# Moving work across tile borders in the first phase of a hybrid decoder layer

## The reference

```
h = rmsnorm(x, g_mix)                       # x * rsqrt(mean(x^2) + eps) * g
z = h @ w_in                                # split into xa, ga, q, k, v (512 columns each)
xa_c = causal_dwconv(xa_ext, conv_a_w, conv_a_b)            # width 4
r, gi = sigmoid(block_diag(xa_c, w_r, b_r)), sigmoid(block_diag(xa_c, w_i, b_i))
a = exp(-8 * r * softplus(-lambda))
u = sqrt(1 - a^2) * gi * xa_c;   hs = scan(h[t] = a[t] * h[t-1] + u[t])
ya = hs * gelu(ga);   q, k = partial_rope(q), partial_rope(k)
```

## Time and profile before

| | |
|---|---|
| median of 3 runs | 3018.76 us (3014.42 to 3021.68) |
| span of the profiled execution | 3016.2 us; its own time outside the profiler is not given, the span is 2.6 us under the median |
| mean granted TensorE clock | 0.969 of full speed |
| TensorE matmul busy | 2880.6 us (96%) |
| VectorE, ScalarE, GpSimd busy | 1738.7 (58%), 1482.5 (49%), 850.4 us (28%) |
| first phase: tile 0 of chunk 0 to the last turn of v | 18.4 to 591.5 us |

### The profile page before, as it was taken

The page is one execution under the profiler, slowest core; times in us unless marked ns, Lnnn a source line. Parts: engine busy times, 40 slices in busy tenths (PEclk is TensorE's granted clock), DMA queues, the critical chain, the costliest instruction groups (busy, mean ns, idle before and its releaser), DMA issues.

```text
span 3016.2 us, 44469 instructions
## 1 busy us (share of the span) xinstructions
PE 2880.6 (96%) x15264; PEld 2717.8 (90%) x15264; DVE 1738.7 (58%) x2949; ACT 1482.5 (49%) x2648; POOL 850.4 (28%) x960
## 2 busy tenths in 40 slices
PE   7898899999999998999999999999999999999998
PEld 6898898867666897999999999999999999999998
DVE  7867767689622675555546555455554555545543
ACT  5565655666655783554334443344433443344431
POOL 4566665545200244111321112111221112211111
PEclk8999999989899998999999999999999999999999
DMA  5344343455444333434434344343533444334332
GB/s 163 98 155 138 109 148 123 139 199 187 156 140 142 102 120 127 119 114 144 131 118 136 113 149 126 113 142 112 155 122 108 145 132 139 114 113 144 114 119 75
DMA packets 151107, 395.26 MB, mean 131 GB/s; under 512 B 19605, under 2 KB 66581, under 8 KB 146821
## 3 DMA queue, kind: packets, MB, share of 16 engines
q1 hardware_dynamic: 114480, 349.69, 37.0%
q10 hardware_dynamic: 34196, 34.58, 3.7%
q0 software_dynamic: 2240, 8.52, 0.7%
HBM read 358.17 MB, written 34.57 MB: 130 GB/s over the span
## 4 chain that ended last, share of the span: by engine, by line
PE 83%; DVE 5%; issue 5%; POOL 2%; ACT 2%; DMA 0%; DVEq 0%; POOLq 0%; ACTq 0%; SPq 0%
PE bank L1523 22%; PE bank L1525 22%; PE bank L1524 22%; PE bank L1594 7%; PE bank L1619 2%; PE bank L1606 2%; PE bank L1682 2%; PE bank L1618 1%; DVE xc L934 1%; DVE pm L1010 0%; DVE d L959 0%; PE bank L1678 0%; PE bank L1679 0%; DVE h_lo L870 0%; POOL sq L1288 0%
## 5 line engine op out<-in xcount | busy, mean ns | idle before, releaser
L857 DVE TENSOR_TENSOR w_lo<-stage,w_hi 128x1024 fp32r<-128x1024 f32 x500 | 652.3, 1305 | 348.0 <-ACT w_hi L471 340.3
L1523 PE MATMUL bank<-hb_hi,w_hi 128*128 128x416 f32 x2240 | 792.4, 354 | 21.4 <-DVE hb_lo L1163 20.2
L471 ACT ACTIVATE w_hi<-stage 128x1024 fp32r<-128x1024 f32 x500 | 527.7, 1055 | 548.8 <-PE bank L1525 529.9
L1525 PE MATMUL bank<-hb_hi,w_lo 128*128 128x416 f32 x2240 | 794.0, 354 | 0.0
L1524 PE MATMUL bank<-hb_lo,w_hi 128*128 128x416 f32 x2240 | 786.1, 351 | 0.0
L1523 PEld LDWEIGHTS bank<-hb_hi,w_hi 128*128 128x128 f32 x2240 | 423.4, 189 | 30.3 <-issue 16.9
L1524 PEld LDWEIGHTS bank<-hb_lo,w_hi 128*128 128x128 f32 x2240 | 424.0, 189 | 7.6 <-issue 0.6
L1525 PEld LDWEIGHTS bank<-hb_hi,w_lo 128*128 128x128 f32 x2240 | 422.9, 189 | 3.0
L1523 PE MATMUL bank<-ff_hi,w_hi 128*128 128x416 f32 x960 | 338.0, 352 | 0.0
L1525 PE MATMUL bank<-ff_hi,w_lo 128*128 128x416 f32 x960 | 337.3, 351 | 0.0
L1524 PE MATMUL bank<-ff_lo,w_hi 128*128 128x416 f32 x960 | 335.4, 349 | 0.0
(11 more groups left out here) (246 smaller groups left out, 4275.0 us busy)
## 6 DMA issues: line engine op xcount, KB each, us to landing
stage<-in_w SPq DMA_DIRECT2D x500, 512.0 KB, 3.6
past<-in_past SPq DMA_DIRECT2D x32, 1152.0 KB, 6.1
vb<-out_v SPq DMA_DIRECT2D x48, 256.0 KB, 2.8
attention_rows<-ob SPq DMA_DIRECT2D x32, 264.0 KB, 2.1
oc<-attention_rows SPq DMA_DIRECT2D x16, 528.0 KB, 3.9
xs<-in_x ACTq DMA_DIRECT2D x40, 208.0 KB, 2.5
qb<-query_rows SPq DMA_DIRECT2D x16, 512.0 KB, 7.8
xT<-in_x ACTq DMA_DIRECT2D x4, 1664.0 KB, 10.1
```

What stands on the lines that cost most here:

```text
L471: e.activation(w_hi[s][:], stage[s % STAGE][:], ACT.Copy).then_inc(hi_ready, 1)
L857: e.tensor_tensor(w_lo[s][:], stage[s % STAGE][:], w_hi[s][:].bitcast(F32), ALU.subtract).then_inc(lo_ready, 1)
L1523: e.matmul(out, w_hi[s][:, k], hi, start=start, stop=False)
L1525: return e.matmul(out, w_lo[s][:, k], hi, start=False, stop=stop)
```

## The change

Only the first phase is touched. The arithmetic is the same, and no DMA is added or taken away.

- TensorE: in tile 19 each step k but the last adds to a new semaphore `h_free`. The gate matmuls of group j stand behind tile 5j+3 instead of 5j+2, and `mean_square` behind tile 13 instead of 11.
- ScalarE: `normed_hi_a` of the next chunk stands, all eight slices together, ahead of group 3's square root (it was behind it, in two parts around the copy of `v_cols`). Slice k waits for `h_free` of step k, the last for the end of tile 19. The copies of q and k out of PSUM stand ahead of the sigmoids, and the root of the norm goes behind group 2's square root.
- VectorE: the scan of group j goes behind `xc_lo` of group j+1 (that of group 3 to the end of the chunk). In group 3, `ahead(c, v_t)` and all eight `normed_lo_a` stand ahead of the reciprocal of `d`; they were behind `a_`. The reciprocal of `rstd` goes to the end of group 2.
- GpSimd: the squares go behind the products that give `gi` of groups 0 and 1.

```
 ScalarE, normed_hi_a                      (h_free is a new semaphore)
                 for k in ks:
                     e.wait_ge(hn_ready, KD * c + k + 1)
+                    if not (isinstance(c, int) and c == 0):
+                        if k < KD - 1:
+                            e.wait_ge(h_free, (KD - 1) * (c - 1) + k + 1)
+                        else:
+                            e.wait_ge(tile_done, c * W_IN)
                     e.activation(h_hi[:, k], xT[:, k], ACT.Identity, ...)
 ScalarE, chunk
-                    if j == 2 and more:
-                        ... (root of the norm into rstd)
                     for i, t in enumerate(qk):
                         ahead(c, t)
+                        b = done(c, t)
+                        if not (first and j == 0):
+                            e.wait_ge(shuffled, 2 * m + i - 1)
+                        e.activation(raw[i][:], b[:, 0:C], ACT.Copy)...
                         if i == 1:
                             e.wait_ge(gates_done, m + 1)
                             ... (sigmoids and tanh)
-                        b = done(c, t)
-                        ... (the copy into raw[i])
                     ahead(c, v_t)
+                    if j == 3 and more:
+                        normed_hi_a(c + 1, range(KD))
                     e.wait_ge(d1_ready, m + 1)
                     e.activation(r_[:], r_[:], ACT.Sqrt, scale=4.0)...
+                    if j == 2 and more:
+                        ... (root of the norm into rstd)
                     b = done(c, v_t)
-                    if j == 3 and more:
-                        normed_hi_a(c + 1, range(3))
                     e.activation(v_cols[:], b[:, 0:C], ACT.Copy)...
-                    if j == 3 and more:
-                        normed_hi_a(c + 1, range(3, KD))
 VectorE, chunk
                     e.tensor_tensor(xc_lo[:], ...)
+                    if j > 0:
+                        scan(c, first, j - 1)
                     ...
                             e.tensor_scalar(d_[j % 2][:], r_[:], 1.0, None, ALU.add)...
                             e.wait_ge(d1_ready, m + 1)
+                            if j == 3 and more:
+                                ahead(c, v_t)
+                                normed_lo_a(c + 1, range(KD))
                             e.reciprocal(d_[j % 2][:], d_[j % 2][:])...
                             ...
-                        if i == 0 and j == 2 and more:
-                            ... (reciprocal of rstd)
-                    if j == 3 and more:
-                        normed_lo_a(c + 1, range(2))
-                    ahead(c, v_t)
-                    if j == 3 and more:
-                        normed_lo_a(c + 1, range(2, KD))
-                    ... (the scan, moved unchanged into scan(c, first, j))
+                    if not (j == 3 and more):
+                        ahead(c, v_t)
+                    if j == 2 and more:
+                        ... (reciprocal of rstd)
+                scan(c, first, JT - 1)
 GpSimd, chunk
-                    if more and j < 2:
-                        square_sum(c + 1, range(KD)[4 * j:4 * j + 4])
                     ...
                     e.tensor_tensor(gi[:], gi[:], d_[j % 2][:], ALU.mult).then_inc(u_ready, 1)
+                    if more and j < 2:
+                        square_sum(c + 1, range(KD)[4 * j:4 * j + 4])
 TensorE, chunk
                         last = product(bank[t % 4][:, 0:C], ...)
+                        if more and t == W_IN - 1 and k < KD - 1:
+                            last.then_inc(h_free, 1)
-                    if t % 5 == 2:
+                    if t % 5 == 3:
                         ... (gate matmuls)
-                    if t == 11 and more:
+                    if t == 13 and more:
                         mean_square(c + 1)
```

More of the change, by code:

```diff
@@ L200, in build @@
         hn_ready, hh_ready, hl_ready = sem("hn_ready"), sem("hh_ready"), sem("hl_ready")
+        h_free = sem("h_free")
         xa_carried, tap0_done, taps, smp_tap = sem("xa_carried"), sem("tap0_done"), sem("taps"), sem("smp_tap")
@@ L574, in chunk @@
                     e.activation(gl[j % 2][:], b[:, 0:C], ACT.Gelu_apprx_tanh).then_inc(evacuated[g_a % 4], 1)
-                    if j == 2 and more:
-                        e.wait_ge(ms_ready, c + 2)
-                        e.wait_ge(hn_ready, KD * (c + 1))
-                        e.activation(rstd[:], bank[4][:, 0:C], ACT.Sqrt, bias=eps[:, 0:1]).then_inc(rms_ready, 1)
                     for i, t in enumerate(qk):
                         ahead(c, t)
+                        b = done(c, t)
+                        if not (first and j == 0):
+                            e.wait_ge(shuffled, 2 * m + i - 1)
+                        e.activation(raw[i][:], b[:, 0:C], ACT.Copy).then_inc(evacuated[t % 4], 1)
                         if i == 1:
@@ L594, in chunk @@
                             e.activation(r_[:], r_[:], ACT.Tanh, scale=sp[:, 0, j:j + 1]).then_inc(t_ready, 1)
-                        b = done(c, t)
-                        if not (first and j == 0):
-                            e.wait_ge(shuffled, 2 * m + i - 1)
-                        e.activation(raw[i][:], b[:, 0:C], ACT.Copy).then_inc(evacuated[t % 4], 1)
                     ahead(c, v_t)
+                    if j == 3 and more:
+                        normed_hi_a(c + 1, range(KD))
                     e.wait_ge(d1_ready, m + 1)
                     e.activation(r_[:], r_[:], ACT.Sqrt, scale=4.0).then_inc(s_ready, 1)
+                    if j == 2 and more:
+                        e.wait_ge(ms_ready, c + 2)
+                        e.wait_ge(hn_ready, KD * (c + 1))
+                        e.activation(rstd[:], bank[4][:, 0:C], ACT.Sqrt, bias=eps[:, 0:1]).then_inc(rms_ready, 1)
                     if not more and j == 3:
@@ L915, in softplus, with scan @@
                 step(e.tensor_copy(sp[:, 0], sp[:, 7]))
+            def scan(c, first, j):
+                m = JT * c + j
+                e.wait_ge(u_ready, m + 1)
+                e.wait_ge(lru_a, m + 1)
+                if first:
+                    v = lambda x: x[:, 0:SMP].rearrange("p (n s) -> p n s", s=SS)
+                    flat = lambda x: x[:].rearrange("p n s -> p (n s)")
+                    e.tensor_copy(a5[:, :, 1:], v(a_)).then_inc(smp_step, 1)
+                    e.tensor_copy(u5[:, :, 1:], v(gi)).then_inc(smp_step, 1)
+                    e.tensor_copy(u5[:, :, 0], h0[:, j]).then_inc(smp_step, 1)
+                    e.wait_ge(smp_step, 6 * j + 3)
+                    e.tensor_tensor_scan(flat(h5), flat(a5), flat(u5), 0.0, ALU.mult, ALU.add).then_inc(smp_step, 1)
+                    e.wait_ge(smp_step, 6 * j + 4)
+                    e.tensor_copy(v(r_), h5[:, :, 1:]).then_inc(smp_step, 1)
+                    e.tensor_copy(hs_o[:, j], h5[:, :, SS]).then_inc(smp_step, 1)
+                    e.wait_ge(smp_step, 6 * j + 6)
+                    e.tensor_tensor_scan(r_[:, SMP:], a_[:, SMP:], gi[:, SMP:], 0.0, ALU.mult, ALU.add).then_inc(h_ready, 1)
+                else:
+                    e.wait_ge(h_carried, m - JT + 1)
+                    e.tensor_tensor_scan(r_[:], a_[:], gi[:], h_car[:, j:j + 1], ALU.mult, ALU.add).then_inc(h_ready, 1)
+                e.wait_ge(h_ready, m + 1)
+                e.tensor_copy(h_car[:, j:j + 1], r_[:, C - 1:C]).then_inc(h_carried, 1)
             def chunk(c, first, more):
@@ L962, in chunk @@
                             e.tensor_scalar(a_[:], d_[j % 2][:], 2.0, -1.0, ALU.mult, ALU.add).then_inc(lru_a, 1)
-                        if i == 0 and j == 2 and more:
-                            e.wait_ge(rms_ready, c + 2)
-                            e.reciprocal(rstd[:], rstd[:]).then_inc(rstd_ready, 1)
-                    if j == 3 and more:
-                        normed_lo_a(c + 1, range(2))
-                    ahead(c, v_t)
-                    if j == 3 and more:
-                        normed_lo_a(c + 1, range(2, KD))
[L972 to L992, removed]
+                    if not (j == 3 and more):
+                        ahead(c, v_t)
+                    if j == 2 and more:
+                        e.wait_ge(rms_ready, c + 2)
+                        e.reciprocal(rstd[:], rstd[:]).then_inc(rstd_ready, 1)
+                scan(c, first, JT - 1)
             chunks(e, chunk)
```

## The result

The changed kernel takes 2999.79 us (median of 4 runs, 2997.18 to 3001.55) against 3016.59 us before (3013.32 to 3021.68): ratio 0.9944 [0.9932, 0.9956]. It is faster by 17 us, where 2972 us and 47 us were forecast; 2949 to 2989 us was the range. The profiled execution has a span of 2999.8 us (before 3016.2) at a mean granted clock of 0.975 (0.969).

The account below looks back on a forecast made before the run. TensorE, busy 96% of 3016.2 us, bounds the kernel; in the first phase it waits for `h_lo` and `xc_lo`. Gains of 36.5 and 12 us less 1.7 make 46.8 us: 2972 us, range 2949 to 2989.

Parts of the forecast that it names:

- Part 1: Inside chunks of the first phase: later gates and mean, moved squares and scan remove all eight `xc_lo` waits; 36.5 us.
- nothing, but thin: Second half of the squares ends some 3 us before the mean behind tile 13, so no cost.
- Part 2: Border between chunks: wait of 2.25 us, then five of 0.83; 7.2 us a border, 12 us gained in all.
- rival A: Border stays as long or gets longer, with L950 standing behind addition and scaling; 2980 to 2992 us; chance 0.24.
- Part 3: Costs: nothing at tile 3 and the gates after the border; 1.7 us lost at the last `v_cols` of the phase.
- rival C: Slower: scan 3 holds up tile 3's `w_lo` and group 0's taps after the border; 3032 us if `gi` is 14 us late; chance 0.04.
- Rival D: No change: the gates' stalls move whole to the border, GpSimd or VectorE setting the length; 3019 us; chance 0.06.
- The sum: 36.5 + 12 - 1.7 = 46.8 us off the 3016.2 us span gives 2969.4; median 2.6 above it: 2972 us.
- the 103 to 106 us: Sign for the whole prediction: windows of chunks 1 to 3 are 103 to 106 us long, or it is wrong.

Follow-up runs that it names:

- the first part alone: The changed kernel with `h_hi` and `h_lo` at the border back in the places of the kernel before, `d` + 1 on VectorE: 3018.26 us, ratio 1.0006.
- the fastest run: The changed kernel with `d` + 1 on ScalarE, eight scalings ahead of group 2's `ya`, group 3's first `gi` product waiting for the eighth `h_lo`: 2959.85 us.

## Why the prediction was wrong

**Part 1, the step that failed.** It listed what is queued behind the sigmoids and the scan that move back as "`ya` on GpSimd and the store of `ya` in its queue". The list stops one engine short. Behind the tanh stands `d` + 1, behind that the root, behind that `v_cols`, and TensorE's turn of v waits for it. I costed `d` + 1 at its old length, "`d` + 1 at 4.1", half a microsecond behind the tanh, and the turns inside a chunk at nothing. In its new place it starts inside one of GpSimd's runs, and 0.36 us become 3.29. The runs price that at 27.2 us (2999.79 with it, 2972.60 without).

**Part 1, "nothing, but thin" for the mean.** It was thin: the mean waits at all four places, 6.8 us. But the cause is the same `d` + 1, since with it on ScalarE no mean waits.

**Part 1, the gates.** All eight waits go, as forecast, and with `d` + 1 free the saving shows: the first phase is then 40.7 us shorter (573.1 - 532.5), and less the 5.9 us of the borders that leaves 34.8, which is 36.5 - 1.7 as forecast. The trail of the earlier trace rows gave the squares a share in the late `xc_lo`; with the gates a tile later their place no longer matters.

**Part 2, the second step that failed.** The border was mis-sized: 12 us forecast, 3.3 measured in the changed kernel. Three of its borders go the way that was forecast, a wait and then turns. But the wait is 3.0 to 3.1 us in place of 2.25, and the slow matmuls stay: tile 20 takes 10.3 to 10.6 us, a cost of 8.8 to 9.2 us a border where I took 7.2. The fourth, into chunk 1, costs 11.4, because `w_lo` stands through the whole run. That is what rival A had for `h_lo` (a wait of 5.5 us and nothing gained); A's own place, L950, did not stand. With `d` + 1 on ScalarE `w_lo` stands at three of the four borders. The wait ahead is then longer than before (5.94 us into chunk 3; 24 us over the four borders against 25), and what is saved is the second wait of 1.17 us inside the tile and some of the slow matmuls behind it (tile 20 takes 6.6 to 7.0 us there). That the 11.5 us between the two orders come close to the 12 forecast is luck: 4 of them are the old border, which had become dearer.

**Part 3.** The turn at the end waits 3.38 us, 1.8 more; forecast 1.7. Tile 3 and the gates of group 0 never wait: rival C did not happen.

**Rival D** came nearest in outcome, that the stalls move on whole, and with the first part alone they do (3018.26 us). Its reason, too much work for GpSimd or VectorE, is not what the runs show: in the fastest run chunks 1 to 3 take 102.3, 101.4 and 101.3 us with the same GpSimd work. I gave it 0.06, on the ground that GpSimd and VectorE are busy for 75 and 87 us of 97. A busy time says how much work an engine has, not how long an instruction will stand; VectorE's own busy time grew by 21 and 18 us in chunks 2 and 3, with the same 90 instructions.

**The sum.** Of the 46.8 us, 14.6 came in the first phase: 3.3 at the border, 11.3 of the 34.8 elsewhere. That 2972.60 us with `d` + 1 free meets the 2972 us forecast is luck: 5.9 us at the border, not 12, and 4.7 of the 45.5 us in the span came after the first phase, which no run here explains. (With the same code there, that stretch took 2420 to 2425 us in the profiles of six kernels.) The windows of its chunks 1 to 3, 112.0, 106.3 and 106.2 us, miss the 103 to 106 us too. And the span lies 1.8 us under the time of its own run (3001.55 against 2999.8), where the sum took 2.6 from the median.

## What to carry to other kernels

When a step moves, follow every engine's queue behind it until TensorE, and ask of each short VectorE instruction on that way what GpSimd will be doing at its new time. Where GpSimd has several products in a row, move the short instruction to ScalarE or make GpSimd wait for it: the one gained 27 us, the other 17, and the first with scaling earlier and one such wait at the border 40. Price two moved parts together; here the first part alone gained nothing where 34.8 us were expected, and the second on top of it 18.5 where 12 were.

## What the runs showed of the hardware

A VectorE instruction can stand behind a row of GpSimd instructions, not only the one in progress: `d` + 1 stood through four (4.84 us at most in the changed kernel) and, with gates and sigmoids alone moved, through eight (8.07 us), `a_` through seven (7.10 us), `w_lo` through eight (9.49 us, into chunk 1 of the changed kernel). In other places the two take turns (eight `h_lo` in 11.13 us beside scaling, 4.58 us alone). What decides between the two is not settled; of those that stand here, `d` + 1 comes behind a shuffle or after idle time, `a_` behind the reciprocal, `w_lo` after idle time or (the 9.49 us) behind `d` + 1, and the `h_lo` that take turns follow one another. That makes no rule: with `d` + 1 on ScalarE, `w_lo` of the border into chunk 1 comes after 1.68 us of idle time and takes 1.89 us.

`d` + 1 and `a_` read one SBUF tile each, and I had taken such instructions for free, from the reciprocal, which kept its 2.75 us beside three GpSimd products. The Trainium skill, SBUF — State Buffer, § Who interferes with whom, says that `tensor_scalar` in a mode with two ports contends with GpSimd. The Trainium skill, VectorE: DVE Perf Modes, § Mode 2×_2P, says that the mode with two ports is for instructions with one source tensor, float32 too, with source and destination in SBUF and an outermost dimension that is even or the same in both (416 columns here). The traces agree for `d` + 1 and `a_` (0.36 and 0.38 us free, 3 to 8 us in a run), and the reciprocal, which is not among the instructions named there, never stood (2.74 to 2.75 us in all 20 of the changed kernel). The first of the two sections speaks of waiting for one whole instruction of the other engine; here `d` + 1 and `a_` waited for four to eight, and the measurement decides.
